# A fused two-block layer on one core: expert-stage tail spread, norm sums with three products, two plain projection pieces

## The reference

```python
# first block
mod = silu(c) @ ada_w + ada_b                       # six shift/scale/gate vectors
u = modulate(rmsnorm(x, norm_mix_g), sh_mix, sc_mix)
p = u @ w_in                                        # conv branch and RWKV branch
x = x + gt_mix * (concat(y_conv, y_rwkv) @ w_out)
u = modulate(rmsnorm(x, norm_ffn_g), sh_ffn, sc_ffn)
x = x + gt_ffn * peer_ffn(u)                        # below
x = rmsnorm(x, final_g)
# peer_ffn: 8 heads, 16 experts of 16384 for each token and head
q = u @ w_q; s = q . sub_keys                       # two halves of 128 keys
expert, best = top16(top16(s0) + top16(s1)); gate = softmax(best)
h = gelu(sum(expert_u[expert] * u)); out = sum(gate * h * expert_v[expert])
# second block
h = rms_norm(x, g_mix_norm_2) * (1 + sc_m) + sh_m
proj = h @ w_in_2                                   # q, k, v, indexer, two gates
x = x + gt_m * (merged(two attentions, gates) @ w_out_2)
h = rms_norm(x, g_ffn_norm_2) * (1 + sc_f) + sh_f
x = x + gt_f * ((silu(g) * u_ff) @ w_down_2)
```

## Time and profile before

| | |
|---|---|
| time, three runs | 1426.35, 1429.79 (median), 1432.38 us |
| the profiled execution | 1435.83 us, its span 1434.0 us |
| busy in the span | PE 1237.9 (86%), DVE 912.6 (64%), ACT 408.7 (28%), POOL 273.6 (19%) |
| DMA | 428.32 MB, mean 299 GB/s |
| mean granted TensorE clock | 0.966 of full |

### The profile page before, as it was taken

How to read it: one execution, slowest core, us unless ns; L and a number is a source line. 1 busy time by engine, 2 the same in 40 slices (tenths; PEclk the granted TensorE clock), 3 DMA queues, 4 the chain that set the end, 5 groups by cost and what they waited for, 6 DMA issues and landing times. The chain is left out here.

```text
span 1434.0 us, 20041 instructions
## 1 busy us (share of the span) xinstructions
PE 1237.9 (86%) x7858; PEld 845.2 (59%) x7858; DVE 912.6 (64%) x2024; ACT 408.7 (28%) x864; POOL 273.6 (19%) x264
## 2 busy tenths in 40 slices
PE   5898998888888878888887777779998999899998
PEld 2888867543333324333332222369995679899998
DVE  0595235697887868787777865764436666555542
ACT  2652225411110201111010110153443363544431
POOL 0000000144443444444344344200000000000000
PEclk8899999989999999999999999989999979999999
DMA  9366079599999999999999999764642744344552
GB/s 396 136 235 184 4 312 427 227 414 421 421 421 421 422 421 416 417 415 415 418 408 421 421 413 422 332 261 177 235 177 118 300 170 176 118 177 176 182 204 114
DMA packets 50766, 428.32 MB, mean 299 GB/s; under 512 B 5744, under 2 KB 7920, under 8 KB 8304
## 3 DMA queue, kind: packets, MB, share of 16 engines
q0 software_dynamic: 36864, 268.45, 45.3%
q1 hardware_dynamic: 13808, 158.59, 28.7%
HBM read 423.64 MB, written 1.05 MB: 296 GB/s over the span
## 5 line engine op out<-in xcount | busy, mean ns | idle before, releaser
L1364 PE MATMUL bank<-arena 128*128 128x512 f32 x1024 | 498.0, 614 | 109.8 <-DVE arena L1526 109.7
L1364 PEld LDWEIGHTS bank<-arena 128*128 128x128 f32 x1024 | 176.4, 190 | 416.6 <-DVE arena L1526 280.3
L1580 DVE CUSTOM_DVE_ANT_0 arena<-arena 128x1024 f32<-128x1024 f32 x256 | 313.4, 1224 | 139.3 <-DMA arena<-experts_in,arena 137.7
L501 PE MATMUL bank<-rounded,rounded 128*128 128x256 f32 x1240 | 365.2, 295 | 39.9 <-DVE rounded L460 26.5
L1284 POOL DMA_INDIRECT arena<-experts_in,arena x256 | 273.1, 1067 | 611.3 <-PE bank L1364 355.3
L502 PE MATMUL bank<-rounded,rounded 128*128 128x256 f32 x1240 | 357.9, 289 | 0.0
L503 PE MATMUL bank<-rounded,ring_r 128*128 128x256 f32 x1240 | 357.6, 288 | 0.0
L478 DVE TENSOR_TENSOR ring_r<-ring,rounded 128x1024 fp32r<-128x1024 f32 (+2 forms) x149 | 187.1, 1266 | 153.9 <-ACT rounded L473 153.6
L501 PEld LDWEIGHTS bank<-rounded,rounded 128*128 128x128 f32 x1240 | 244.0, 197 | 46.8 <-issue 39.6
L502 PEld LDWEIGHTS bank<-rounded,rounded 128*128 128x128 f32 x1240 | 244.1, 197 | 3.0 <-issue 2.9
L503 PEld LDWEIGHTS bank<-rounded,ring_r 128*128 128x128 f32 x1240 | 244.1, 197 | 0.0
(11 more groups left out here) (250 smaller groups left out, 959.2 us busy)
## 6 DMA issues: line engine op xcount, KB each, us to landing
ring<-slots_in SPq DMA_DIRECT2D x68, 2048.0 KB, 8.1
arena<-slots_in SPq DMA_DIRECT2D x4, 2048.0 KB, 23.6
arena<-experts_in,arena POOLq DMA_INDIRECT x256, 13.6
xT<-xT_in SPq DMA_DIRECT2D x1, 1024.0 KB, 10.8
mixT<-slots_in SPq DMA_DIRECT2D x1, 1024.0 KB, 12.3
out_dram<-xT SPq DMA_DIRECT2D x1, 1024.0 KB, 4.8
arena<-slots_in SPq DMA_DIRECT2D x1, 896.0 KB, 7.0
uT<-arena SPq DMA_DIRECT2D x4, 142.0 KB, 9.3
```

The costliest lines, as they stand in the source:

```text
L501: pe.matmul(dst, hi[:, k, :], xh, start=(k == 0), stop=False)
L1364: ins = pe.matmul(psum[2 * tt + half][:, :], diag[:, r % DIAGS, :], rows[:, r % GRING, D + 512 * half:D + 512 * half + 512], start=(h == 0 ...
L1580: dve.tensor_tensor_reduce(rows[:, r % GRING, 0:D], rows[:, r % GRING, 0:D], utok[:, tt, :], 1.0, 0.0, ALU.mult, ALU.add, hdot[:, r:r + 1] ...
```

## The change

It merges four edits. In the last head, the copy, flips, additions and squares of tile 0 come earlier, and its sums are spread over rows 23 to 30, one `k` ahead of each; the squares with the gain are divided, four tiles on VectorE, four on ScalarE (as `Square` with a scale, so half of `fgsq` holds another constant); the roots are computed per token tile and lie in `mixT`. In the residual blocks with sums, VectorE adds up the squares of tiles 0 to 5, and TensorE makes three products with ones, not eight; the third piece of `following` is prepared after the last tile. In the second input projection, items 0 and 1 are made by plain products as each shifted tile becomes ready, and the split starts at item 2.

```diff
+        SUMMED = 6
+        def dve_add_square(dve, k):
+
+            dve.wait_ge(nm_sq, KT * norms[0] + k + 1)
+            if k > 1:
+                dve.wait_ge(nm_part, parts[0] * (SUMMED - 1) + k - 1)
+            dve.tensor_tensor(uT[:, 0, :], uT[:, 0, :], uT[:, k, :], ALU.add).then_inc(nm_part, 1)
+
+        def pe_sum_rest(pe):
+
+            pe.wait_ge(nm_part, (parts[0] + 1) * (SUMMED - 1))
+            pe.matmul(psum[0][:, 0:T], ones, uT[:, 0, :], start=True, stop=False)
+            for k in range(SUMMED, KT):
+                pe.wait_ge(nm_sq, KT * norms[0] + k + 1)
+                ins = pe.matmul(psum[0][:, 0:T], ones, uT[:, k, :], start=False, stop=(k == KT - 1))
             ins.then_inc(nm_ms, 1)
...
+        PLAIN = 2
+
+        def plain_pieces(pe, n, mm):
+            wait_slot(pe, n)
+            for k in range(KT):
+                pe.wait_ge(nm_shift, shifted[0] + k + 1)
+                for i in range(PLAIN):
+                    ins = pe.matmul(psum[i][:, 0:T], slot(n)[:, k, i * P:(i + 1) * P], uT[:, k, :],
+                                    start=(k == 0), stop=(k == KT - 1))
+                    if k == KT - 1:
+                        ins.then_inc(mm, 1)
...
-                v(dve.tensor_scalar(fgsq[:, :], vcol("final_g", 0, 8), 1.0 / D, None, ALU.mult))
-                v(dve.tensor_tensor(fgsq[:, :], fgsq[:, :], vcol("final_g", 0, 8), ALU.mult))
+                v(dve.tensor_scalar(fgsq[:, 0:4], vcol("final_g", 0, 4), 1.0 / D, None, ALU.mult))
+                v(dve.tensor_tensor(fgsq[:, 0:4], fgsq[:, 0:4], vcol("final_g", 0, 4), ALU.mult))
+                v(dve.tensor_scalar(fgsq[:, 4:8], vcol("final_g", 4, 4), D ** -0.5, None, ALU.mult))
...
# residual_block, ScalarE (VectorE alike)
-                        if following and i >= len(tiles) - 3:
-                            n = i - len(tiles) + 3
-                            following.act_prime(act, n, n + 1)
+                        if following and i in (5, 6):
+                            following.act_prime(act, i - 5, i - 4)
...
+                    if following:
+                        following.act_prime(act, 2)
...
+                        if squares and 2 <= i < SUMMED + 1:
+                            dve_add_square(dve, i - 1)
...
-        roots = area(27692, 2, T)
+        roots = mixT[:, 0:2, :]
...
# expert rows, TensorE
-                            if h == HEADS - 1 and n == 24:
+                            if h == HEADS - 1 and n == 20:
                                 out_flips(0)
-                            if h == HEADS - 1 and n == 31:
-                                out_sums(0)
+                            if h == HEADS - 1 and 23 <= n < 31:
+                                out_sum(0, n - 23)
+                                out_gsum(0, n - 23)
...
-                out_sums(1)
+                for k in range(KT):
+                    out_sum(1, k)
+                for k in range(KT):
+                    out_gsum(1, k)
...
# ScalarE
+                    for k in range(GSQ_DVE, KT):
+                        act.activation(gsq[:, k, half_tile(tt)], xT[:, k, half_tile(tt)], ACT.Square,
+                                       scale=fgsq[:, k:k + 1]).then_inc(px_gsqa, 1)
...
-                            if h == HEADS - 1 and n == 20:
+                            if h == HEADS - 1 and n == 18:
                                 act.wait_ge(rows_used, TILE0_DONE)
...
-                            if h == HEADS - 1 and n == 30:
+                            if h == HEADS - 1 and n == 22:
                                 squares(0)
...
-                act.wait_ge(px_var, 2)
-                act.activation(roots[:, :, :], roots[:, :, :], ACT.Ln).then_inc(nm_rstd, 1)
-                act.wait_ge(nm_rstd, 2 * norms[0] + 1)
-                act.activation(roots[:, :, :], roots[:, :, :], ACT.Exp, scale=-0.5).then_inc(nm_rstd, 1)
+                for tt in range(TT):
+                    act.wait_ge(px_var, 2 * tt + 2)
+                    act.activation(roots[:, :, half_tile(tt)], roots[:, :, half_tile(tt)], ACT.Ln).then_inc(px_ln, 1)
+                    act.wait_ge(px_ln, tt + 1)
+                    ins = act.activation(roots[:, :, half_tile(tt)], roots[:, :, half_tile(tt)], ACT.Exp, scale=-0.5)
+                ins.then_inc(nm_rstd, 2)
...
# VectorE: variances(tt) holds the two operations of before for one tile;
# add_out(0) at n = 21 (26), gain_squares(0) at n = 22 (28) with GSQ_DVE = 4 tiles (8)
                 make_diag(*before)
+                variances(0)
                 dve.wait_ge(rows_used, NROW)
...
-        wi2 = Split([(SLOTS["w_in2"][0] + items[n][1], 512, items[n][2], n) for n in i2_feat], KT, uT, 11552, i2_mm)
+        wi2 = Split([(SLOTS["w_in2"][0] + items[n][1], 512, items[n][2], n) for n in i2_feat[PLAIN:]], KT, uT, 11552, i2_mm)
...
+                plain_pieces(pe, s0, i2_mm)
                 for n, (kind, s, col, *_) in enumerate(items):
-                    if n == 0 or items[n - 1][1] != s:
+                    if n < PLAIN:
+                        continue
+                    if items[n - 1][1] != s:
                         wait_slot(pe, s0 + s)
...
-                    if kind == "feat":
-                        wi2.act_hi(act, i2_feat.index(n) + LEAD)
+                    if kind == "feat" and n >= PLAIN:
+                        wi2.act_hi(act, i2_feat.index(n) - PLAIN + LEAD)
...
-                for i in range(LEAD, len(i2_feat)):
-                    wi2.dve_lo(dve, i)
-                    if i in (4, 6):
-                        dve_token(dve, 2, i // 6)
+                for i in range(LEAD + PLAIN, len(i2_feat)):
+                    wi2.dve_lo(dve, i - PLAIN)
+                    if i in (5, 6):
+                        dve_token(dve, 2, i - 5)
```

More of the change, by code:

```diff
@@ L283, in dve_mod @@
                                      ALU.add)
-        nm_sq, nm_ms, nm_rstd, nm_n, nm_shift = (sem("nm_" + x) for x in ("sq", "ms", "rstd", "n", "shift"))
+        nm_sq, nm_ms, nm_rstd, nm_n, nm_shift, nm_part = (sem("nm_" + x) for x in ("sq", "ms", "rstd", "n", "shift", "part"))
+        SUMMED = 6
+        parts = [0]
         shifted = [0]
@@ L1154, in _ @@
                     if squares:
-                        pe_sum_squares(pe)
+                        pe_sum_rest(pe)
                 @block.scalar
@@ L1185, in _ @@
                         sp3.dve_lo(dve, i + LEAD)
-                        if following and i >= len(tiles) - 3:
-                            n = i - len(tiles) + 3
-                            following.dve_prime(dve, n, n + 1)
+                        if following and i in (5, 6):
+                            following.dve_prime(dve, i - 5, i - 4)
                         dve.wait_ge(mm, i + 1)
@@ L1191, in _ @@
                                                  ALU.mult, ALU.add).then_inc(ev, 1)
+                        if squares and 2 <= i < SUMMED + 1:
+                            dve_add_square(dve, i - 1)
                         if i == len(tiles) - 1 or tiles[i + 1][0] != s:
                             dve.sem_inc(slot_used[(s0 + s) % RING], 1)
+                    if following:
+                        following.dve_prime(dve, 2)
+            parts[0] += 1 if squares else 0
         eight = [(i // 4, (i % 4) * P) for i in range(8)]
@@ L1261, in half_tile @@
             return slice(tt * P, tt * P + P)
+        px_gsqa, px_ln = sem("px_gsqa"), sem("px_ln")
+        GSQ_DVE = 4
         TILE0_DONE = row_of(HEADS - 1, 0, TOPK - 1) + 1
@@ L1313, in out_flips, with out_sum, out_gsum @@
                         ins.then_inc(px_mm, 1)
-                def out_sums(tt):
-                    for k in range(KT):
-                        pe.wait_ge(px_sq, KT * tt + k + 1)
-                        pe.matmul(psum[0][:, half_tile(tt)], ones, uT[:, k, half_tile(tt)],
-                                  start=(k == 0), stop=(k == KT - 1))
-                        pe.wait_ge(px_gsq, KT * tt + k + 1)
-                        ins = pe.matmul(psum[1][:, half_tile(tt)], ones, gsq[:, k, half_tile(tt)],
-                                        start=(k == 0), stop=(k == KT - 1))
-                    ins.then_inc(px_ms, 1)
+                def out_sum(tt, k):
+                    pe.wait_ge(px_sq, KT * tt + k + 1)
+                    pe.matmul(psum[0][:, half_tile(tt)], ones, uT[:, k, half_tile(tt)],
+                              start=(k == 0), stop=(k == KT - 1))
+                def out_gsum(tt, k):
+                    if k < GSQ_DVE:
+                        pe.wait_ge(px_gsq, GSQ_DVE * tt + k + 1)
+                    else:
+                        pe.wait_ge(px_gsqa, (KT - GSQ_DVE) * tt + k - GSQ_DVE + 1)
+                    ins = pe.matmul(psum[1][:, half_tile(tt)], ones, gsq[:, k, half_tile(tt)],
+                                    start=(k == 0), stop=(k == KT - 1))
+                    if k == KT - 1:
+                        ins.then_inc(px_ms, 1)
                 pe_mod(pe, 3, 0, 2)
```

(21 more changed lines are left out.)

1 line of the change is left out of this document (added).

## The result

The changed kernel takes 1422.32 us, the median of 13 runs (1419.07 to 1425.99), against 1429.79 for the kernel before, also the median of 13 (1426.35 to 1435.65): a ratio of 0.9949, interval 0.9935 to 0.9963, or 7.3 us less (5.3 to 9.3). The forecast was 1422.0. The profiled execution took 1421.9 us, its span 1420.1.

A forecast was written before the change was run, and what follows sets the result against it. Full DMA bounds the expert stage, TensorE the second input projection, a serial tail lies between; -3.5 - 2.1 - 2.4 + 0.5 - 0.35 + 0.1 = -7.75 us, median 1429.8 to 1422.0, range 1417.0 to 1427.5.

The forecast's parts named there:

- Part 1: End of the expert stage: tile 0's sums moved out of the tail to rows 23 to 30, gain 3.5 us.
- Rival (c): Expert stage's end: inserted sums don't catch up, the tail's two gains fall to 2.4 and 1.5, 1423.8 us; chance 0.08.
- a last dot product later than its start: Expert stage: prediction wrong if the last dot product is later than before by more than its start.
- Part 2: After the last expert row: copy to norm 7.75 us instead of 9.87, gain 2.1 (1.5 to 2.4).
- Part 3: Second input projection's start: two plain pieces, third piece at +10.8 after the norm, low clock for 4 us, gain 2.4.
- Part 4: Norm sums with three products after both output projections: +0.5 us first, -0.35 second, +0.1 for scale constants.
- The extra operation for the scale constants: Small VectorE operation, at most 0.2 us in a stage where TensorE leads; counted as 0.1 us lost.
- (a): Clock kept at the plain pieces (gain 4.4 us) and keys early (up to 1.9): 1417.7 us; chance 0.23 in part or whole.
- (b): Low clock through the plain pieces (+2.4 us) and under head 0's scores (0.95 lost): 1427.3 us; chance 0.17.
- Rival (d): Second input projection: split pieces after the plain ones run low too, 2.24 us lost each; 1438.5 with five; chance 0.04.
- the profile's extra 6 us: The profiled execution of the kernel before was 6 us above the median; nothing said the parts scale with it.

The follow-up runs named there:

- this part alone: The kernel before with only the second input projection's edits (items 0 and 1 as plain products): 1425.96 us, ratio 0.9969.
- the kernel with all edits: The changed kernel plus the keys' load requested early and unread filler products in two TensorE gaps: 1417.92 us, on another chip 1416.41.

## Why the prediction held, step by step

**Part 1 (3.5 us).** Measured 3.57. The catching-up can be read on GpSimd's gather issues, kernel after:

```profile
906.93 1.00 POOL L1321 DMA_INDIRECT arena<-experts_in,arena  x1 [1.50 <-PE bank L1407]
909.53 1.61 POOL L1321 DMA_INDIRECT arena<-experts_in,arena  x1 [1.59 <-PE bank L1407]
912.90 0.95 POOL L1321 DMA_INDIRECT arena<-experts_in,arena  x1 [1.77 <-PE bank L1407]
...
917.52 0.94 POOL L1321 DMA_INDIRECT arena<-experts_in,arena  x1 [1.23 <-PE bank L1407]
```

With a period of 2.48 us the issue after 906.93 + 2 x 2.48 = 911.89 comes 1.0 late, as foretold (1.1), and the last one 0.7 late (917.52 against 916.85). The last dot still waits 0.97 us for its gather, the same as before: the stream of gathers didn't notice. Rival (c) is out. One step was mis-sized on the safe side: the passes of a row with its two pairs start 2.16 us apart (915.37 and 917.53 on TensorE) and not 2.33, because the 1.88 us listed for four passes hold their pipelined end (the next pass starts 1.72 us after the first, at 917.09); TensorE catches up 0.32 per row, twice as fast as forecast. The prediction named a last dot product later than its start as a sign of being wrong, and from the first gather to the last dot it was indeed 653.96 us for 652.20. This is scatter: five profiles without the tail's edits give 651.4 to 653.7, mean 652.3, nine with them 651.1 to 654.0, mean 652.2.

**Part 2 (2.1 us).** Measured 1.90: norm 7.97 after the copy, not 7.75. The working had the sums done at 6.0 and the variances right behind; VectorE's first variance starts at 941.79, 6.09 after the copy, and the norm 1.88 later where 1.74 had been added up. Dependent short operations cost somewhat more than their own lengths: the last Ln, 0.42 long, starts at 942.43 and the Exp behind it 0.51 later. The term's own lower bound (1.5) had named this.

**Part 3 (2.4 us).** The mechanism was right, the sizes were off. TensorE started at +1.57 (forecast +1.8), the passes took 6.79 us at the full level (6.96), and the low stretch held 3.4 us and cost 1.68 (4 and 2.0), so the third piece came at +10.05, not +10.8: 3.15 us of gain in the profile. The total of this part alone, -4.4 (-6.1 to -2.7), holds both values. What the prediction lacked is that the low stretch is no fixed price of a gap: it fell in four of five profiles with the same 3.49 us, and its length was 3.4 or 6.8 us. The Trainium skill, TensorE: Matmul & The Clock Gate, section "Why this matters for your kernels", was weighed ahead of the result: idle time between bursts brings the half rate back. By that rule the low level was due: the trace agrees in four of these profiles and disagrees in the one without the sums. The same page, in "Part 1: The HAM clock gate (the "warmup" mystery)", says of the start of a kernel that the number of slow matmuls differs from run to run of one kernel; the 10.05 and 11.2 us of kernels with identical code there agree.

**Part 4 (+0.5 - 0.35 + 0.1).** At the first place the root came 1.73 us earlier (forecast 1.9) and all of it vanished behind the keys' load: SyncE issued that load at 251.7 (before 255.0) and it landed 12.8 us later (12.3), so 35.1 us after the projection's first addition and 35.2 before; all nine profiles with this load in its old place give 35.1 to 35.6. The early keys on top of the change brought the scores forward, which shows the cause. The cost of the clock at the scores was expected between 0 and 0.95: five profiles with the sums and the late keys give 36.49, 37.44, 37.69, 37.91 and 37.31 us to the first top-k operation, mean 37.4, four of them with low scores; four without give 36.60, 36.67, 36.65 and 36.78, mean 36.7. That is +0.7 for +0.5. At the second place 23.36 against 23.91 is -0.55 in the profile of the kernel after, but the nine profiles with the edit scatter from 23.35 to 23.97 (mean 23.5) and the five without from 23.65 to 23.91 (mean 23.75), so the size of -0.35 is not tested. The prediction lacked a term here: the sums end earlier while the block waits for the third weight piece, and TensorE is idle for longer before the feed-forward's first product, first before, then after:

```profile
1231.61 0.55 PE L501 MATMUL bank<-rounded,rounded 128*128 128x256 f32 x1 [5.26 <-DVE rounded L460]
```

```profile
1218.27 0.55 PE L530 MATMUL bank<-rounded,rounded 128*128 128x256 f32 x1 [6.70 <-DVE rounded L489]
```

The low stretch there held 6.8 us in all five profiles without the edit, 10.2 in four of the six with it and no fill; the third piece started 11.6 to 12.1 us after the norm without (mean 11.85) and 11.7 to 12.4 with (mean 12.15). So about 0.3 us is paid behind the place where about 0.2 is gained. The extra operation for the scale constants could not be seen.

**The sum.** -7.75 against 7.3 (5.3 to 9.3) measured. The pieces by the traces, with the means for Part 4: -3.57 - 1.90 - 3.15 + 0.7 - 0.2 + 0.3 = -7.8. Part 3 gave 0.75 more than forecast; Part 2 (0.2) and Part 4 (some 0.6) gave less, so the errors cancel. That the median came within 0.4 us of the forecast, with 2 us of uncertainty on it and a clock draw of 1.7 us inside Part 3, is luck. Rivals (a) and (b) were each half seen, and by luck of the clock: the run without the sums had (a)'s clock, and low scores, one half of (b), came in four of five profiles. Rival (d) did not occur: after 3.4 or 6.8 us the level was always back. That the medians would move by the sum of the stretches while one profile moves by 13.9 us also held; the forecast rightly took nothing from the profile's extra 6 us.

## To carry to other kernels

Split a serial tail at the last transfer that it waits for, and price each step from the rows before it: here three stretches were each good to 0.75 us, and the sum lay well inside the measured interval of 5.3 to 9.3. A gain at a place that waits for a DMA behind a backlog is worth nothing until that DMA is moved; once moved, the gain was there in the trace (1.56 us), though not in every total. An early load of 1 MB and fills of idle TensorE time together gave 4 to 6 us more than the merged change. Where an idle gap of TensorE stood before dense work, a few unread products in it turned a draw of the clock (8.37, 10.05 or 11.2 us to the third piece in five profiles) into one time (8.37 in all three with the fill).

## What was not expected of the hardware

Low stretches fall in dense work too. In the kernel after, with TensorE busy throughout:

```profile
997.70:1001.10 3.40, 3.40 (x32) 3.40 (x32) 0.00 (x0) 0.97 (x3) 0.00 (x0) 1.00 0.82 352
1001.20:1004.40 3.20, 3.20 (x17) 3.20 (x16) 1.23 (x1) 0.24 (x1) 0.00 (x0) 0.50 1.01 338
```

Seventeen passes in the second stretch where the first has 32. What ran before it is on TensorE's timeline:

```profile
996.80 3.38 PE L1742 MATMUL bank<-ring,uT 128*128 128x8 f32 x29
1000.04 0.36 PE L530 MATMUL bank<-rounded,rounded 128*128 128x256 f32 x1
```

3.4 us of products with only 8 columns count as busy in the profile, and a low stretch follows soon after. It costs 1.5 us: from the third piece to the end of the second input projection it is 104.8 to 105.0 us with it and 103.3 to 103.5 without. It was there in nine of the fourteen profiles (in one of them 6.8 us low, and 106.0), each time beginning 2.7 to 4.8 us after the first of the narrow products, and absent from both profiles of the kernel with all edits, from the kernel before and from those with the sums alone and with sums and early keys. No edit reaches that place, so by these runs it is chance whether it comes; that the narrow products bring it was not tested. In the profile of the sums alone a low stretch of 3.4 us fell into the sums of the expert stage's tail: 11.50 us from copy to norm, where the four other profiles with the same code show 9.87.

Summed over a whole execution the low level held 100 us in the profile of the kernel before (span 1434.0), 80 in that of the kernel after (1420.1), 59 without the sums (1414.4) and 56 in the second profile of the kernel with all edits (1410.2). The kernel after and the one without the sums differ by 5.7 us in their spans and by 1.4 in their medians: how much of an execution falls to the low level is a scatter that no edit of this size can be read against in one profile.
